# Two-block transformer kernel on one core: another order for the first transfers

## The chip, the cores and the metric

The kernel runs on one core of one Trainium2 chip. The metric is the device time of one execution in microseconds; three runs of the kernel before gave 947.91, 948.18 and 948.75 us, so the median is 948.18 us. A profile was taken of one further execution, which took 949.62 us; its recorded span is 947.6 us, and 2.0 us lie around the span.

## The reference

A sequence of 256 tokens with 1024 features goes through a first block and then through a second block of two layers, all in float32. Only the head of the first block matters for this change:

```
u = rms_norm(x, norm_g)                    # norm_g: the first of the "norm weights"
proj = u @ w_in                            # values v, queries q, keys k, convolution and gate columns
s = q k^T / 8 + alibi bias, softmax, times v   (16 heads)
y_conv = (silu(zc) * bg * conv3(cg * xc)) @ w_out_conv
gates  = sigmoid(g + b_merge)
h = x + (gate_c * y_conv + gate_a * y_attn) @ w_o ;  rms_norm(h, final_g)
```

The second block (memory attention, compressed, windowed and block attention with relative position bias, two convolutional feed-forward parts) follows, with further small tables: a one-hot of distances and the relative bias, the convolution taps of the feed-forward, the position embedding and the second matrix of the compression.

## The kernel before

Every weight comes as a block of 128 partitions by 1024 float32 (512 KB) out of one long tensor, `stream`. A block is loaded into a buffer `raw`, copied by ScalarE into a rounded upper part `wh` (`make_high`, L463), and VectorE writes the rest, `raw - wh`, into `wl` (`make_low`, L895). TensorE then makes three products for each pair: upper by upper, upper by lower, lower by upper. The activations are split in the same way into `xh` and `xl`. In this part of the kernel there are three `raw`, three `wh` and three `wl` buffers (RING = 3).

Nothing plans the order at run time: each engine has its own list of instructions, written out by hand, and semaphores tie them together. `split_l` counts the blocks that VectorE has split, `split_h` those that ScalarE has copied, `used` those that TensorE has finished. SyncE (SP) issues most transfers. It starts block b+3 when `split_l` says that block b has left its `raw` buffer. GpSimd (POOL) issues the bias of each head pair (`alibi`) and the norm's rows (`load_gb`).

The head of the program, in order:

- SP issues two halves of x (L311), the transposed norm weights `gbt` (L312), the first three weight blocks (L307), and seven small tables (L315 to L321): `convw` 16 KB, `bm` 8 KB, `onehot` 66 KB, `relb` 1.5 KB, `convf` 88 KB, `pe_kv` 16 KB, `w2` 128 KB. Each of the seven raises one semaphore, `consts_in`, by 16.
- TensorE warms up with products of zeros (L1720), transposes x (L1728), warms up again, and begins the stage "value rows": eight blocks, k = 0 to 7, each with four 512-column products of each kind (L1742, L1745, L1748).
- ScalarE squares x (L514), waits for `gbt`, and then rounds columns of the transposed x (`raw_high`, L523) between the copies of blocks 0, 1 and 2. Behind these stand L539 (a copy of a broadcast), the wait `consts_in >= 16 * 7` (L540), a small copy of the merge bias `bm` (L541), and only then the loop that copies block 3 and all later ones.
- VectorE scales the transposed x by `gbt` (`raw_fetch`, L1071), which is what `raw_high` reads.
- POOL makes the norm's reciprocal roots, issues the first bias (`alibi(0)`, L381) and the final norm's row (`load_gb(a["final_g"])`, L373), then waits for the finished values (L393).

TensorE also waits for all seven tables, but only behind the eight value blocks (L1760). The first bias is read by the first head pair's scores; the final row is read hundreds of microseconds later.

Of the kernel before, what the change touches and what calls it, by code (L numbers as in the profile page):

```python
# [47 lines left out]
RING = 3  # L48
# [47 lines left out]
def slot_of(b):  # L96
    if b in EXTRA:
        return EXTRA[b]
    return (b - sum(e < b for e in EXTRA)) % RING
# [14 lines left out]
B_DEEP = B_KM0  # L114


def home_of(b):

    if b < B_DEEP:
        return b % RING  # L120
    m = (b - B_DEEP) % DEEP
    return RING + m if m < RING else (B_DEEP + m) % RING
# [32 lines left out]
def build_program(nc, a):  # L155
    ctx = ExitStack()
    with ctx:
        def sb(name, shape, dt=F32):
            return ctx.enter_context(nc.sbuf_tensor("sb_" + name, shape, dt))

        def sem(name):
            return ctx.enter_context(nc.semaphore(name))
# [27 lines left out]
        gbt = sb("gbt", [P, 10, KT])  # L190
# [57 lines left out]
        split_h, split_l, used = sem("split_h"), sem("split_l"), sem("used")  # L248
        gains_in, kv_free = sem("gains_in"), sem("kv_free")
# [27 lines left out]
        def norm_wait(engine, nm, what, count):  # L277
            before = norms.index(nm) - first_norm.get(what, 0)
            engine.wait_ge(S[nm, what], before * per_norm[what] + count)
# [24 lines left out]
        @block.sync  # L304
        def _(sp):
            def load(b, home):
                sp.dma_start(raw[home][:, :, :], a["stream"][bass.ds(b, 1)].rearrange(  # L307
                    "a p (k c) -> p (a k) c", k=KT)).then_inc(landed[home], 16)

            for t in range(NT):  # L310
                sp.dma_start(x_tok[:, t, :], a["x"][0, t * P:(t + 1) * P, :]).then_inc(x_in[t], 16)  # L311
            sp.dma_start(gbt[:, :, :], a["gains_t"]).then_inc(gains_in, 16)  # L312
            for b in range(RING):
                load(b, slot_of(b))
            sp.dma_start(convw[:, :, :], a["conv_t"]).then_inc(consts_in, 16)  # L315
            sp.dma_start(bm[:, :, :], a["b_merge_t"]).then_inc(consts_in, 16)
            sp.dma_start(onehot[:, :], a["distance_hot"]).then_inc(consts_in, 16)
            sp.dma_start(relb[0:32, :], a["rel_bias_2"]).then_inc(consts_in, 16)
            sp.dma_start(convf[:, :, :, :], a["conv_f_t"]).then_inc(consts_in, 16)
            sp.dma_start(pe_kv[:, :, :], a["pe_t"]).then_inc(consts_in, 16)  # L320
            sp.dma_start(w2[:, :, :, :], a["w2_t"]).then_inc(consts_in, 16)  # L321

            with sp.Fori(1, B_DEEP // RING) as i:
                for n in range(RING):
                    sp.wait_ge(split_l, i * RING + (n - RING + 1))
                    load(i * RING + n, n)
            for b in range(B_DEEP // RING * RING, B_DEEP):
                sp.wait_ge(split_l, b - RING + 1)
                load(b, home_of(b))
            for b in range(B_DEEP, B_DEEP + DEEP):  # L330
                if b == B_DEEP:
                    sp.wait_ge(S["p2", "free_a"], KT // 2)
                if b == B_DEEP + 2:
                    sp.wait_ge(S["p2", "free_a"], KT)
                if b >= B_DEEP + RING:
                    sp.wait_ge(split_l, b - DEEP + 1)
                load(b, home_of(b))
            count = (N_BLOCKS - B_DEEP) // DEEP
            with sp.Fori(1, count) as i:
                for n in range(DEEP):  # L340
                    b = B_DEEP + n
                    sp.wait_ge(split_l, i * DEEP + (b - DEEP + 1))
                    load(i * DEEP + b, home_of(b))
            for b in range(B_DEEP + count * DEEP, N_BLOCKS):
                sp.wait_ge(split_l, b - DEEP + 1)
                load(b, home_of(b))
            for t in range(NT):
                norm_wait(sp, "n5", "z", 2 * t + 2)
                sp.dma_start(a["out"][0, t * P:(t + 1) * P, :], x_tok[:, t, :]).then_inc(out_done, 16)
            sp.wait_ge(out_done, 16 * NT)  # L350
# [3 lines left out]
        def _(pool):  # L354
# [9 lines left out]
            def rstd(nm, t, eps):  # L364

                norm_wait(pool, nm, "var", t + 1)
                chain.link(pool.tensor_scalar(st[:, 8 + t:9 + t], st[:, 6 + t:7 + t], 1.0 / D, eps,
                                              ALU.mult, ALU.add))
                pool.tensor_tensor(st[:, 10 + t:11 + t], st[:, 8 + t:9 + t], half[:, :],
                                   ALU.pow).then_inc(S[nm, "rstd"], 1)  # L370

            def load_gb(gain, shift):
                pool.dma_start(gb[:, 0, :], gain.partition_broadcast(P)).then_inc(gb_in, 16)  # L373
                if shift is not None:
                    pool.dma_start(gb[:, 1, :], shift.partition_broadcast(P)).then_inc(gb_in, 16)

            def alibi(i):

                if not isinstance(i, int) or i:
                    pool.wait_ge(S["p1", "max"], i * 4)  # L380
                pool.dma_start(bias[:, :, 0:T], a["alibi"][bass.ds(i, 1)].rearrange(  # L381
                    "a p (h c) -> p (a h) c", h=2)).then_inc(S["p1", "bias_in"], 16)

            for t in range(NT):
                rstd("n0", t, EPS_RMS)
            alibi(0)
            load_gb(a["final_g"], None)

            def pick_values(i):

                if not isinstance(i, int) or i:
                    pool.wait_ge(S["p1", "o"], i)
                pool.tensor_copy(v_s[:, :, :], v_all[:, :, bass.ds(i * P, P)]).then_inc(v_pair, 1)  # L393

            pool.wait_ge(v_up[0], 2)
            pick_values(0)

            pool.wait_ge(rel_sb, 1)
            pool.dma_start(rel_rows, relf[:, :]).then_inc(rel_out, 16)
# [57 lines left out]
        def _(act):  # L457
# [51 lines left out]
                                   accum_out=den[:, c:c + 1]).then_inc(S[ph, "exp"], 1)  # L509


            for t in range(NT):
                act.wait_ge(x_in[t], 16)
                act.activation(z[:, t, :], x_tok[:, t, :], ACT.Square,  # L514
                               accum_out=st[:, 6 + t:7 + t]).then_inc(S["n0", "var"], 1)
# [1048 lines left out]
        def _(pe):  # L1564
# [169 lines left out]
            def value_rows(k):  # L1734

                parts = [(xh[:, k, t * P:(t + 1) * P], xl[:, k, t * P:(t + 1) * P],
                          *(w[slot_of(k)][:, 4 * n:4 * n + 4, :].rearrange("p k c -> p (k c)") for w in (wh, wl)),
                          bank[4 + 2 * t + n]) for t in range(NT) for n in range(2)]
                pe.wait_ge(split_h, k + 1)
                norm_wait(pe, "n0", "xh", k + 1)  # L1740
                for th, _, hw, _, bk in parts:
                    pe.matmul(bk[:, :], th, hw, start=k == 0, stop=False)  # L1742
                norm_wait(pe, "n0", "xl", k + 1)
                for _, tl, hw, _, bk in parts:
                    pe.matmul(bk[:, :], tl, hw, start=False, stop=False)  # L1745
                ready(k + 1)
                for th, _, _, lw, bk in parts:
                    last = pe.matmul(bk[:, :], th, lw, start=False, stop=k == KT - 1)  # L1748
                last.then_inc(used, 1)
# [536 lines left out]
```

## Time and profile before

| | |
|---|---|
| median of 3 runs | 948.18 us (947.91 to 948.75) |
| profiled execution, its own time | 949.62 us |
| its span | 947.6 us |
| TensorE busy | 927.2 us, 98% |
| VectorE busy | 664.2 us, 70% |
| ScalarE busy | 529.2 us, 56% |
| GpSimd busy | 65.5 us, 7% |
| moved by DMA | 173.02 MB, mean 183 GB/s |

The busy shares are means over the whole span. The change touches only the first 36 us, so what counts is the order of events there: the chain of waits, the list of instructions by time, and the time from a transfer's issue to its landing.

### The profile page before, as it was taken

How to read it: one execution, taken by the hardware profiler on the slowest of the kernel's cores; microseconds unless marked ns; L12 is line 12 of the kernel's file. 1: busy time of each engine (PE TensorE's matmuls, PEld its weight loads, DVE VectorE, ACT ScalarE, POOL GpSimd, SP SyncE). 2: the span in 40 equal slices, each digit the busy share in tenths (PEclk: the TensorE clock that was granted, in tenths of full speed). 3: DMA queues.
4: the chain of work that ended last, by engine and by line, in shares of the span. 5: the costliest groups of instructions: out<-in, count | busy, mean ns of one | idle time of the engine just before them, and what ended most of it. 6: DMA issues, size and time to landing. Idle time of an engine off the chain costs nothing.

```text
span 947.6 us, 19722 instructions
## 1 busy us (share of the span) xinstructions
PE 927.2 (98%) x7025; PEld 845.9 (89%) x7030; DVE 664.2 (70%) x1286; ACT 529.2 (56%) x976; POOL 65.5 (7%) x116
## 2 busy tenths in 40 slices
PE   8999999999999999999999999999999999999995
PEld 6899999999999988667999999998988799999995
DVE  6666666566767877886786566677677886666666
ACT  6545555555544657764655455565665565555553
POOL 1000000000000002640000000001000100000001
PEclk9999999999999999999999999999999999999998
DMA  7655555557556565315366655555554546565641
GB/s 261 194 186 188 188 174 179 180 176 239 193 185 206 216 228 189 118 62 171 134 209 223 198 197 185 192 200 166 195 184 157 178 155 228 193 197 179 199 156 45
DMA packets 48235, 173.02 MB, mean 183 GB/s; under 512 B 6031, under 2 KB 6479, under 8 KB 48060
## 3 DMA queue, kind: packets, MB, share of 16 engines
q1 hardware_dynamic: 44732, 159.78, 50.4%
q0 software_dynamic: 3456, 12.61, 4.4%
q8 instruction: 30, 0.49, 0.2%
q14 instruction: 17, 0.14, 0.0%
HBM read 171.29 MB, written 1.07 MB: 182 GB/s over the span
## 4 chain that ended last, share of the span: by engine, by line
PE 89%; DVE 5%; ACT 3%; issue 1%; DMA 1%; POOL 0%; POOLq 0%; SPq 0%; DVEq 0%; ACTq 0%
PE bank L1575 18%; PE bank L1576 18%; PE bank L1574 18%; PE ysum L1645 6%; PE ysum L1647 6%; PE ysum L1646 6%; PE bank L1696 2%; DVE sb_wl L895 2%; PE ysum L1703 1%; PE ysum L1710 1%; ACT sb_wh L463 1%; PE ysum L1742 1%; PE ysum L1748 1%; PE ysum L1745 1%; PE ysum L1574 1%
## 5 line engine op out<-in xcount | busy, mean ns | idle before, releaser
L1575 PE MATMUL bank<-sb_xl,sb_wh 128*128 128x256 f32 x1360 | 378.1, 278 | 0.0
L1576 PE MATMUL bank<-sb_xh,sb_wl 128*128 128x256 f32 x1360 | 376.0, 276 | 0.0
L1574 PE MATMUL bank<-sb_xh,sb_wh 128*128 128x256 f32 x1332 | 370.7, 278 | 0.0
L895 DVE TENSOR_TENSOR sb_wl<-sb_raw,sb_wh 128x1024 fp32r<-128x1024 f32 x196 | 239.2, 1223 | 109.0 <-ACT sb_wh L463 107.6
L1576 PEld LDWEIGHTS bank<-sb_xh,sb_wl 128*128 128x128 f32 x1360 | 255.5, 188 | 0.0
L1575 PEld LDWEIGHTS bank<-sb_xl,sb_wh 128*128 128x128 f32 x1360 | 255.5, 188 | 0.0
L1574 PEld LDWEIGHTS bank<-sb_xh,sb_wh 128*128 128x128 f32 x1332 | 250.3, 188 | 5.0 <-issue 2.7
L463 ACT ACTIVATE sb_wh<-sb_raw 128x1024 fp32r<-128x1024 f32 x196 | 205.8, 1055 | 87.2 <-PE bank L1576 39.2
L895 DVE TENSOR_TENSOR sb_wl<-sb_gates,sb_wh 128x1024 fp32r<-128x1024 f32 x63 | 76.9, 1220 | 9.7 <-ACT sb_wh L463 9.7
L1645 PE MATMUL ysum<-sb_wh,sb_mh 128*128 128x512 f32 x208 | 81.3, 391 | 0.1
L1646 PE MATMUL ysum<-sb_wl,sb_mh 128*128 128x512 f32 x208 | 81.1, 390 | 0.0
L1647 PE MATMUL ysum<-sb_wh,sb_ml 128*128 128x512 f32 x208 | 81.0, 390 | 0.0
L463 ACT ACTIVATE sb_wh<-sb_gates 128x1024 fp32r<-128x1024 f32 x63 | 66.3, 1052 | 4.4 <-PE ysum L1626 2.3
L789 ACT ACTIVATE sb_t_a<-bank,sb_convf 128x256 f32<-128x256 f32 x44 | 24.9, 565 | 74.1 <-PE bank L1576 69.8
L1469 DVE SCALAR_TENSOR_TENSOR sb_t_a<-bank,sb_convf,sb_t_a 128x255 f32<-128x255 f32 x44 | 21.2, 482 | 43.1 <-ACT sb_t_a L789 43.1
L508 ACT ACTIVATE sb_pr<-sb_sc,sb_mx 128x128 f32<-128x128 f32 x80 | 35.4, 445 | 25.0 <-DVE sb_mx L1046 25.0
L895 DVE TENSOR_TENSOR sb_wl<-sb_t_dg,sb_wh 128x1024 fp32r<-128x1024 f32 x32 | 39.1, 1223 | 10.9 <-ACT sb_wh L463 10.9
L1647 PEld LDWEIGHTS ysum<-sb_wh,sb_ml 128*128 128x128 f32 x208 | 39.1, 188 | 8.3
L1645 PEld LDWEIGHTS ysum<-sb_wh,sb_mh 128*128 128x128 f32 x208 | 39.0, 188 | 8.2 <-issue 1.0
L1646 PEld LDWEIGHTS ysum<-sb_wl,sb_mh 128*128 128x128 f32 x208 | 39.0, 188 | 7.1
L463 ACT ACTIVATE sb_wh<-sb_t_dg 128x1024 fp32r<-128x1024 f32 x32 | 33.9, 1060 | 11.8 <-PE bank L1576 5.7
L1575 PE MATMUL bank<-sb_mixl,sb_wh 128*128 128x256 f32 x128 | 35.6, 278 | 0.0
(308 smaller groups left out, 1497.3 us busy)
## 6 DMA issues: line engine op xcount, KB each, us to landing
sb_raw<-in_stream SPq DMA_DIRECT2D x201, 512.0 KB, 3.4
sb_gates<-in_stream SPq DMA_DIRECT2D x66, 512.0 KB, 3.3
sb_t_dg<-in_stream SPq DMA_DIRECT2D x33, 512.0 KB, 4.2
sb_bias<-rel_rows POOLq DMA_DIRECT2D x12, 384.0 KB, 3.9
sb_bias<-in_alibi POOLq DMA_DIRECT2D x8, 256.0 KB, 3.1
sb_gb<-in_ln_g POOLq DMA_DIRECT2D x4, 512.0 KB, 4.9
sb_gb<-in_ln_b POOLq DMA_DIRECT2D x4, 512.0 KB, 7.2
sb_x_tok<-in_x SPq DMA_DIRECT2D x2, 512.0 KB, 3.7
```

Of the source, the lines that this page charges most:

```text
L463: act.activation(wh[slot_of(b) if slot is None else slot][:, :, :], raw[home_of(b)][:, :, :], ACT.Copy).then_inc(split_h, 1)
L508: act.activation(to[:, branch, h, cols], src, ACT.Exp, bias=mx[:, c:c + 1], scale=-1.0, accum_out=den[:, c:c + 1]).then_inc(S[ph, "exp"], 1)
L789: act.activation(t_a[:, :], bank[2 * c][:, 0:T], ACT.Identity, bias=convf[:, layer, bass.ds(i, 1), 3], scale=convf[:, layer, bass.ds(i, 1), 2]
L895: dve.tensor_tensor(wl[slot][:, :, :], raw[home_of(b)][:, :, :], wh[slot][:, :, :].bitcast(F32), ALU.subtract).then_inc(split_l, 1)
L1469: cf.link(dve.scalar_tensor_tensor(out=t_a[:, 1:T], in0=bank[2 * c][:, 0:T - 1], scalar=convf[:, layer, bass.ds(i, 1), 1], in1=t_a[:, 1:T] ...
L1574: pe.matmul(out, wh[slot][:, k, :], mov_h(k), start=k == 0, stop=False)
L1575: pe.matmul(out, wh[slot][:, k, :], mov_l(k), start=False, stop=False)
L1576: last = pe.matmul(out, wl[slot][:, k, :], mov_h(k), start=False, stop=k == KT - 1)
L1645: pe.matmul(out, th[:, t * P:(t + 1) * P], hw, start=start, stop=False)
L1646: pe.matmul(out, th[:, t * P:(t + 1) * P], lw, start=False, stop=False)
L1647: last = pe.matmul(out, tl[:, t * P:(t + 1) * P], hw, start=False, stop=stop)
L1696: last = pe.matmul(outs[h][:, cols], q[r, t * P:(t + 1) * P], k[r, 0:lead + (t + 1) * P], start=True, stop=True)
```

## The change

- The transfer of `gbt` leaves SP's list and becomes ScalarE's first instruction.
- SP's fourth, fifth and sixth weight loads are written out ahead of the loop (which now begins at 2 in place of 1), each with the same wait as before. The seven tables now stand between and behind them: `convw` and `bm` behind the fourth load, `onehot` and `relb` behind the fifth, `convf`, `pe_kv` and `w2` behind the sixth.
- POOL waits for `used >= 2` before it issues the first bias.
- POOL issues the final norm's row behind its first copy of values (L393) in place of before it.

The waits for `consts_in` (L540 and L1760) are as they were.

```
-            sp.dma_start(gbt[:, :, :], a["gains_t"]).then_inc(gains_in, 16)
             for b in range(RING):
                 load(b, slot_of(b))
+
+            sp.wait_ge(split_l, 1)
+            load(RING, 0)
             sp.dma_start(convw[:, :, :], a["conv_t"]).then_inc(consts_in, 16)
             sp.dma_start(bm[:, :, :], a["b_merge_t"]).then_inc(consts_in, 16)
+            sp.wait_ge(split_l, 2)
+            load(RING + 1, 1)
             sp.dma_start(onehot[:, :], a["distance_hot"]).then_inc(consts_in, 16)
             sp.dma_start(relb[0:32, :], a["rel_bias_2"]).then_inc(consts_in, 16)
+            sp.wait_ge(split_l, 3)
+            load(RING + 2, 2)
             sp.dma_start(convf[:, :, :, :], a["conv_f_t"]).then_inc(consts_in, 16)
             sp.dma_start(pe_kv[:, :, :], a["pe_t"]).then_inc(consts_in, 16)
             sp.dma_start(w2[:, :, :, :], a["w2_t"]).then_inc(consts_in, 16)
 
-            with sp.Fori(1, B_DEEP // RING) as i:
+            with sp.Fori(2, B_DEEP // RING) as i:
...
             for t in range(NT):
                 rstd("n0", t, EPS_RMS)
+            pool.wait_ge(used, 2)
             alibi(0)
-            load_gb(a["final_g"], None)
...
             pool.wait_ge(v_up[0], 2)
             pick_values(0)
+            load_gb(a["final_g"], None)
...
+            act.dma_start(gbt[:, :, :], a["gains_t"]).then_inc(gains_in, 16)
             for t in range(NT):
                 act.wait_ge(x_in[t], 16)
```

## Rows read from the trace of the kernel before

**Rows 1.** Page, part 1: busy us (share of the span) xinstructions, by engine.
```profile
PE 927.2 (98%) x7025; PEld 845.9 (89%) x7030; DVE 664.2 (70%) x1286; ACT 529.2 (56%) x976; POOL 65.5 (7%) x116
```

**Rows 2.** Waits of TensorE, whole span: us in total, times, longest.
```profile
PE ysum L1742 <- ACT sb_wh L463: 1.5, 1, 1.5
```

**Rows 3.** Chain that ended last, in order of time: start us, us, what.
```profile
2.26 6.75 DMA sb_raw<-in_stream
9.03 1.07 ACT sb_wh L463
10.14 1.21 PE ysum L1742 x4
...
18.21 0.92 PE ysum L1748 x4
19.13 0.91 PE ysum L1742 x4
20.05 0.92 PE ysum L1745 x4
```

**Rows 4.** Instructions in order of time, SP: start us, us, engine line op.
```profile
1.79 0.42 SPq L312 DMA_DIRECT2D sb_gbt<-in_gains_t  x1
...
6.15 0.49 SPq L319 DMA_DIRECT2D sb_convf<-in_conv_f_t  x1
...
7.22 0.45 SPq L321 DMA_DIRECT2D sb_w<-in_w_t  x1
11.52 47.08 SPq L307 DMA_DIRECT2D sb_raw<-in_stream  x18
```

**Rows 5.** Instructions in order of time, ScalarE and VectorE (brackets: idle before, releaser).
```profile
7.70 0.88 DVE L1071 TENSOR_SCALAR sb_pt<-bank,sb_gbt 128x256 f32<-128x256 f32 x2 [5.63 <-DMA sb_gbt<-in_gains_t]
...
14.97 1.22 DVE L895 TENSOR_TENSOR sb_wl<-sb_raw,sb_wh 128x1024 fp32r<-128x1024 f32 x1
...
15.95 0.20 ACT L541 ACTIVATE sb_bmh<-sb_bm 128x16 f32<-128x16 f32 x1
...
16.19 1.06 ACT L463 ACTIVATE sb_wh<-sb_raw 128x1024 fp32r<-128x1024 f32 x1
```

**Rows 6.** Instructions in order of time, TensorE's two warm-ups.
```profile
2.31 2.31 PE L1720 MATMUL bank<-sb_zeros 128*128 128x512 bf16 x5 [2.31 <-POOL sb_t_b L361]
...
7.36 1.24 PE L1720 MATMUL ysum<-sb_zeros 128*128 128x512 bf16 x5
```

**Rows 7.** DMA issues, 0 to 40 us: xcount, KB each, median us from issue to landing.
```profile
sb_raw<-in_stream SPq DMA_DIRECT2D x15, 512.0 KB, 4.3
...
sb_gb<-in_final_g POOLq DMA_DIRECT2D x1, 512.0 KB, 6.0
sb_bias<-in_alibi POOLq DMA_DIRECT2D x1, 256.0 KB, 5.8
...
sb_gbt<-in_gains_t SPq DMA_DIRECT2D x1, 40.0 KB, 5.9
rel_rows<-sb_sc POOLq DMA_DIRECT2D x1, 24.0 KB, 1.8
```

**Rows 8.** Weight loads alone: first three (0 to 4 us), then the sixth (15 to 17).
```profile
DMA to landing us min/median/max: 6.7/7.5/8.6
...
DMA to landing us min/median/max: 4.3/4.3/4.3
```

**Rows 9.** Busy by stretch: PE, PEld, DVE, ACT, POOL, granted PE clock, DMA share, GB/s.
```profile
6.00:7.00 1.00, 1.00 (x7) 1.00 (x6) 0.00 (x0) 0.74 (x2) 0.46 (x2) 1.00 0.89 334
...
940.00:942.00 2.00, 0.00 (x0) 0.00 (x0) 2.00 (x3) 0.36 (x2) 1.47 (x2) 1.00 0.00 0
942.00:943.00 1.00, 0.00 (x0) 0.00 (x0) 0.67 (x1) 0.00 (x0) 1.00 (x1) 0.55 0.00 0
```

**Rows 10.** Instructions in order of time, POOL, 5 to 50 us.
```profile
35.92 0.54 POOL L399 DMA_DIRECT2D rel_rows<-sb_sc  x1 [0.42 <-DVE sb_sc L1121]
45.45 0.73 POOL L381 DMA_DIRECT2D sb_bias<-in_alibi  x1 [8.98 <-DVE sb_mx L1046]
```

More of the change, by code:

```diff
@@ L311, in _ @@
                 sp.dma_start(x_tok[:, t, :], a["x"][0, t * P:(t + 1) * P, :]).then_inc(x_in[t], 16)
-            sp.dma_start(gbt[:, :, :], a["gains_t"]).then_inc(gains_in, 16)
             for b in range(RING):
                 load(b, slot_of(b))
+            sp.wait_ge(split_l, 1)
+            load(RING, 0)
             sp.dma_start(convw[:, :, :], a["conv_t"]).then_inc(consts_in, 16)
             sp.dma_start(bm[:, :, :], a["b_merge_t"]).then_inc(consts_in, 16)
+            sp.wait_ge(split_l, 2)
+            load(RING + 1, 1)
             sp.dma_start(onehot[:, :], a["distance_hot"]).then_inc(consts_in, 16)
             sp.dma_start(relb[0:32, :], a["rel_bias_2"]).then_inc(consts_in, 16)
+            sp.wait_ge(split_l, 3)
+            load(RING + 2, 2)
             sp.dma_start(convf[:, :, :, :], a["conv_f_t"]).then_inc(consts_in, 16)
@@ L321, in _ @@
             sp.dma_start(w2[:, :, :, :], a["w2_t"]).then_inc(consts_in, 16)
-            with sp.Fori(1, B_DEEP // RING) as i:
+            with sp.Fori(2, B_DEEP // RING) as i:
                 for n in range(RING):
@@ L385, in _ @@
                 rstd("n0", t, EPS_RMS)
+            pool.wait_ge(used, 2)
             alibi(0)
-            load_gb(a["final_g"], None)
             def pick_values(i):
@@ L396, in _ @@
             pick_values(0)
+            load_gb(a["final_g"], None)
             pool.wait_ge(rel_sb, 1)
@@ L509, in exps @@
                                    accum_out=den[:, c:c + 1]).then_inc(S[ph, "exp"], 1)
+            act.dma_start(gbt[:, :, :], a["gains_t"]).then_inc(gains_in, 16)
             for t in range(NT):
```

## The prediction

> **What bounds the kernel now.** I read the page first. TensorE is busy for 98% of the span [rows 1], so nearly everything that delays it reaches the end, and little else does. The list of its waits then shows only one that this change could shorten: 1.5 us before the first value product, put down to ScalarE's copy of weight block 0 [rows 2]. The chain of waits tells what stands behind it. Block 0's load is issued at 2.26 us and takes 6.75 us, ScalarE copies it from 9.03, and TensorE starts at 10.14 [rows 3]. From there the pieces join without a gap: the products of k = 2 end at 19.13, those of k = 3 begin there, and the lower products L1745 of k = 3 follow at 20.05 [rows 3]. So two questions decide. How much earlier than 10.14 does the stage begin, and does any engine that feeds it come late before its eight blocks are done? Anything further on is paced by TensorE and moves with it.
>
> The instructions in order of time show the second question's weak place. ScalarE's small copy of the merge bias (L541) runs at 15.95, and the copy of block 3 starts at 16.19, 0.24 us later [rows 5]. Ahead of L541 stands the wait for all seven tables. SP had issued the last of them, `w2`, at 7.22 [rows 4], so they were there in time. TensorE needs block 3 at 19.13; the copy ends at 17.25, so 1.9 us of slack cover it.
>
> **The start: the norm weights leave SP's queue.** SP spends 0.42 us on the issue of `gbt`, and with the gap 0.47 us pass until the first weight load, 1.79 to 2.26 [rows 3, 4]. That much block 0's issue moves forward. VectorE's 5.6 us wait for `gbt` [rows 5] goes too, but it isn't what ends last: ScalarE waited for block 0 after its first `raw_high`. The tables, 324 KB by the tile shapes, were issued from 3.68 to 7.7 us and shared the engines with the first three loads. These took 6.7, 7.5 and 8.6 us to land against a median of 4.3 over the head [rows 7, 8]. I call the gain of TensorE's start g.
>
> - Lower bound: -0.2, if block 0's landing is set by the bytes ahead of it (x and `gbt` are still moved first) and `gbt`'s small pieces now slow x.
> - Upper bound: 1.5, since TensorE's second warm-up ends at 7.36 + 1.24 = 8.60 [rows 6] and nothing of the stage can begin earlier (10.14 - 8.60).
> - I take 0.7: 0.47 for the issue and 0.2 for the two thirds of the tables that were moved before 9.0 us, some 200 KB, of which perhaps a third delayed block 0 at 334 GB/s [rows 9].
>
> The issue on ScalarE costs about as much as on SP, 0.4 us, and lies in the time in which ScalarE waits for x anyway.
>
> **The tables: what is late next.** In the new order `convf`, `pe_kv` and `w2` are issued behind the sixth load, and that waits until VectorE has split block 2. The wait on ScalarE (L540) still asks for all seven. Step by step, with g = 0.7:
>
> 1. VectorE's split of block 2 ended at 14.97 + 1.22 = 16.19 [rows 5]; now 15.5.
> 2. SP issues a load 0.2 us behind the split that frees its buffer (the split of block 0 follows its copy, 10.10 [rows 3] + 1.22 = 11.3; the load started at 11.52 [rows 4]): 15.7.
> 3. The load takes 0.35 of SP and a gap of 0.05; from the start of `convf` to the start of `w2` it is 7.22 - 6.15 = 1.07 us [rows 4]. So `w2` is issued at 17.2.
> 4. `w2` lands L later. Nothing in the trace shows a transfer of 128 KB by itself. The nearest rows are a 24 KB transfer, 1.8 us, and weight loads of 512 KB at 4.3 us [rows 7, 8]; these are the two ends. With the sixth load and three tables (744 KB) and the delayed first bias (256 KB, issued at nearly the same moment) 1.0 MB go out between 15.7 and the landing. At 334 GB/s [rows 9] that is 3.0 us of moving, with about 1 us before the first byte and 0.5 behind the last: 20.2. So L = 3.0, midway between the ends.
> 5. ScalarE: the bias copy, and 0.24 later the copy of block 3, 20.44 to 21.50 [rows 5].
> 6. TensorE starts 0.05 behind such a copy and its first piece from a stand took 1.21 us in place of 0.91 [rows 3]: L1745 of k = 3 at 21.55 + 1.21 = 22.75, where it was at 20.05.
>
> The sum is +2.7 us. In general it is L + 0.4 - g: the slack of 1.9 us is used up whatever L is, as the tables are issued so late.
>
> The Trainium skill, "DMA: Bandwidth & Descriptors", section "Anatomy of one DMA — SWDGE (gpsimd) path", gives a transfer a fixed part of about 2.0 us and its bytes at 436 GB/s. That is measured on GpSimd's path; for the 744 KB from the issue of the sixth load it would be an estimate of 3.7 us, the tables in at 19.4, and a sum of +1.9. The 24 KB row at 1.8 us agrees with the fixed part; the 512 KB rows at 4.3 (where it gives 3.2) are above it, and I stay with the rows.
>
> **Behind the stall** the queue on ScalarE is: block 3, scaled column 0, block 4, scaled column 1, and so on. ScalarE needs about 1.06 + 0.4 us and gaps for each pair against TensorE's 2.75 per block, and blocks 4 and 5 have landed by then, so it has caught up within one block. VectorE's split of block 3 ends at 22.8; TensorE wants it 1.9 us after its restart, at 23.4. SP's seventh load waits for that split and goes at 22.9; with 4.3 us it is there at 27.2 and is wanted at 28.7. I count nothing more.
>
> **The first bias and the final row.** The wait `used >= 2` ends at about 15.7, and behind it on POOL stand only the copy of values, just ahead of 35.92 [rows 10], and what follows. The first bias took 5.8 us to land [rows 7]; the next bias is asked for at 45.45, right after the first one's last reader [rows 10], so it has over 20 us of cover. Without that cover it would cost up to 5.8. The final row (512 KB, 6.0 us [rows 7]) is now issued about 35.5, puts 0.6 us ahead of the `rel_rows` transfer at 35.92 [rows 10], which is read only in the second block, and shares the engines with a weight load that has some 6 us from issue to use. Nothing, or at worst 1 us. Taking both out of 7.6 to 14.5 us speeds the fourth load, which nobody waits for now.
>
> **The sum against the times.** The profiled execution took 949.62 us; with +2.7 it is 952.3. The median stands 1.44 below the profiled one, so I expect 950.9.
>
> **The rivals.**
>
> - *The tables are fast, the start is good* (not slower). Place: the landing of `w2`. With L = 1.8 as the 24 KB transfer and g = 1.5 the same steps give +0.7, 948.9 us. For it: the loads are queued and `w2` may be moved beside them; the first loads' 6.7 us shows how crowded the start is. Against it: 512 KB stand ahead in the same queue. It decides where L - g falls below 1.5, or 2.2 us for L at g = 0.7. Chance 0.15. To be faster than before, L would have to be under g - 0.4, which no transfer here shows: 0.03, about 946.
> - *TensorE's clock falls in the new gap.* TensorE would stand from 18.4 to 21.5, 3.1 us. After its last matmul at 938.0 the granted clock is still 1.00 up to 942 and 0.55 in the next us [rows 9], that is, it falls to 1.2 GHz of 2.4 after some 4 us; after the 1.5 us gap at the start the products ran at full rate. Price: the first warm-up of 512-column products took 2.31 us for five, the second 1.24 [rows 6], so the slow stretch lasted between 2.3 and 5.05 us (until 7.36), and half of it is lost: 1.2 to 2.5 more, 952.1 to 953.4 us. Chance 0.08; the gap is shorter than the one that was seen to lower the clock. The Trainium skill, "TensorE: Matmul & The Clock Gate", Part 1, says that the throttled state is the default and activity releases it, which is what the two warm-ups show.
> - *The final row collides at 36 us*, where one weight load comes late: +1, 951.9 with the rest. 0.02.
>
> **Numbers.** The forecast has 0.72, of which 0.06 ends within 0.2%. A change of 0.2%, 1.9 us, is about the least that can be told from none. Slower by more: 0.66 + 0.08 + 0.02 = 0.76; within: 0.06 + 0.15 = 0.21; faster: 0.03. The forecast's own range runs from L = 2.0 at g = 1.0 (+1.4) to L = 4.3 at g = 0.4 (+4.3), 949.6 to 952.5. Taking in part of the fast rival and of the clock's, I give 949.1 to 952.6.
>
> **What would show it.** Right: in the profile after, ScalarE's L541 stands at 19 to 21 us with a wait for a table's transfer of 3 us or more before it, TensorE has one gap of about 3 us before the L1742 of k = 3, and its first L1742 starts at 9 to 9.8. Step 1 is wrong if that start stays at 10.1. Step 4 is wrong if L541 runs before 17.5. The whole is wrong if TensorE shows no gap between k = 2 and k = 3, or if a second gap follows at k = 6 or at 36 to 45 us.

## The result and the profile after

Six runs of the changed kernel took 951.13, 951.61, 953.60, 953.86, 954.29 and 954.85 us, median 953.73; six of the kernel before have a median of 948.46. The ratio is 1.0048 with a 95% interval of 1.0035 to 1.0062: slower by 3.3 to 5.9 us. The forecast was 950.9 with a range of 949.1 to 952.6, so the direction was right and the time lies 1.1 us above the range. Three executions of the experiments below took several times as long as the others (two of the kernel before, one of e10) and are left out of every range and ratio below and of e10's median.

The runs fall in two groups, and with them goes the mean granted clock of TensorE that each run lists: the share of full speed at which the engine was allowed to run, over the whole span. It is 0.997 in the two runs under 952 and 0.996 to 0.993 in the four above 953. The profiled execution is the fastest of the six (951.13 us, span 949.4), so by itself it shows only part of the loss. A second profile of the same kernel, taken in the experiments, was of the second group (954.58 us, span 952.8). Both are needed.

The page of the first, part 1 (busy us, share of the span, instructions); it answers to [rows 1]:

```profile
PE 927.1 (98%) x7030; PEld 844.7 (89%) x7030; DVE 664.3 (70%) x1286; ACT 529.0 (56%) x976; POOL 67.5 (7%) x116
```

The work of TensorE, VectorE and ScalarE is the same within 0.2 us; TensorE's weight loads show 1.2 us less and GpSimd 2.0 more. No engine on the chain does more work, so what was added is waiting. The waits of TensorE and of ScalarE from 12 to 24 us (us in total, times, longest):

```profile
PE ysum L1750 <- ACT sb_wh L470: 3.9, 2, 3.6
...
ACT sb_bmh L549 <- DMA sb_w<-in_w_t: 5.3, 1, 5.3
```

L1750, L1753 and L1756 are the three kinds of value products that were L1742, L1745 and L1748; L470 is the copy of a weight block, L549 the copy of the merge bias. The first line answers to [rows 2]: the 1.5 us wait has become 0.38 at the start and 3.56 ahead of k = 3. The second is new and names the cause, the landing of `w2`. The chain of waits of the same profile, in order of time, answers to [rows 3]:

```profile
1.33 4.54 DMA sb_x_tok<-in_x
...
13.44 1.15 DVE sb_wl L903
14.60 0.35 SPq L307
14.99 0.43 SPq L325
15.47 0.44 SPq L326
15.95 3.73 DMA sb_w<-in_w_t
19.71 0.23 ACT sb_bmh L549
19.96 1.06 ACT sb_wh L470
21.06 1.20 PE ysum L1750 x4
22.26 0.91 PE ysum L1753 x4
```

It reads as the forecast's steps 1 to 6, in their order. The split of block 2 ends at 14.59, the sixth load goes out at 14.60, the tables behind it, `w2` at 15.95; 3.73 us later ScalarE may copy the bias, then block 3, and TensorE goes on at 21.06. The lower products of k = 3 begin at 22.26, where they began at 20.05 [rows 3]: +2.2 us, of which the span keeps 1.8 (949.4 against 947.6).

At the front, the instructions in order of time show the first products starting 1.6 us before those of [rows 3], and the same block of k = 3 behind its gap (brackets: idle before, releaser):

```profile
8.52 1.20 PE L1750 MATMUL ysum<-sb_wh,sb_xh 128*128 128x512 f32 x4 [0.38 <-ACT sb_wh L470]
...
21.06 1.20 PE L1750 MATMUL ysum<-sb_wh,sb_xh 128*128 128x512 f32 x4 [3.56 <-ACT sb_wh L470]
```

### The profile page after: what moved, and what is told of

Its sections match the earlier page's. It is cut to its first block, busy times and chain, and to the rows that moved or that the text cites. A ratio compares the mean times of both kernels' runs of the same rounds, so it can differ in the third digit from the quotient of the medians.

```text
span 949.4 us, 19717 instructions
## 1 busy us (share of the span) xinstructions
PE 927.1 (98%) x7030; PEld 844.7 (89%) x7030; DVE 664.3 (70%) x1286; ACT 529.0 (56%) x976; POOL 67.5 (7%) x116
## 4 chain that ended last, share of the span: by engine, by line
PE 88%; DVE 6%; ACT 3%; issue 1%; DMA 1%; POOL 0%; SPq 0%; POOLq 0%; DVEq 0%; ACTq 0%
PE bank L1583 18%; PE bank L1584 18%; PE bank L1582 18%; PE ysum L1653 6%; PE ysum L1655 6%; PE ysum L1654 6%; DVE sb_wl L903 2%; PE bank L1704 2%; PE ysum L1711 1%; PE ysum L1718 1%; ACT sb_wh L470 1%; PE ysum L1582 1%; PE ysum L1583 1%; PE ysum L1584 1%; ACT sb_xh L503 1%
## 5 line engine op out<-in xcount | busy, mean ns | idle before, releaser
L470 ACT ACTIVATE sb_wh<-sb_raw 128x1024 fp32r<-128x1024 f32 x196 | 205.7, 1055 | 87.1 <-PE bank L1584 39.2
L470 ACT ACTIVATE sb_wh<-sb_gates 128x1024 fp32r<-128x1024 f32 x63 | 66.3, 1053 | 4.4 <-PE ysum L1634 2.3
L1477 DVE SCALAR_TENSOR_TENSOR sb_t_a<-bank,sb_convf,sb_t_a 128x255 f32<-128x255 f32 x44 | 21.2, 482 | 43.1 <-ACT sb_t_a L797 43.1
L470 ACT ACTIVATE sb_wh<-sb_t_dg 128x1024 fp32r<-128x1024 f32 x32 | 33.9, 1060 | 11.8 <-PE bank L1584 5.7
```

The costliest lines, as they stand in the source:

```text
L470: act.activation(wh[slot_of(b) if slot is None else slot][:, :, :], raw[home_of(b)][:, :, :], ACT.Copy).then_inc(split_h, 1)
L1477: cf.link(dve.scalar_tensor_tensor(out=t_a[:, 1:T], in0=bank[2 * c][:, 0:T - 1], scalar=convf[:, layer, bass.ds(i, 1), 1], in1=t_a[:, 1:T] ...
```

## The experiments

Theory C: the stall costs its length in every run, and in most runs the granted clock also falls in it. Rival T: the transfer of `w2` lands later in most runs than in the profiled one. All kernels below were timed beside the kernel before; its medians were 948.69 us (beside a0, e1, e2, e3), 948.63 (b0, e4, e5, e6) and 948.48 (e7 to e10). The last four were timed on another chip than the first eight, so a comparison across the two goes by the ratio to the kernel before as well as by the time.

### The changed kernel again (a0_again), no edit

> The changed kernel once more, unedited. Its six runs so far are 951.1, 951.6, 953.6, 953.9, 954.3 and 954.9 us with a mean granted clock of 0.997 in the first two and 0.993 to 0.996 in the others; its profile (951.13) has the gap of 3.6 us ahead of the k = 3 products and no lower clock in it. Theory C (clock): the gap costs 2.2 us net in every run, and in most runs the granted clock falls in the gap as well, which costs 2 to 3.5 us more. Then the runs fall in two groups, near 951 with clock 0.997 and near 954 with less, and a profile of the second kind shows slow products behind the gap. Theory T (transfer): w2 lands 2 to 3.5 us later in most runs than in the profiled one, and the clock has little to do with it. Then a profile near 954 shows a gap of 6 us or more.

Measured: median 954.70 us (953.92 to 955.09), ratio 1.0063 (1.0051 to 1.0075), clock 0.993 or 0.994 in all six. Theory C expected two groups again, near 951 and near 954; only the second was seen. The chain of its profile:

```profile
16.58 3.94 DMA sb_w<-in_w_t
20.78 1.06 ACT sb_wh L470
21.89 2.08 PE ysum L1750 x4
23.97 1.71 PE ysum L1753 x4
25.68 1.71 PE ysum L1756 x4
27.38 1.26 PE ysum L1750 x4
28.64 0.93 PE ysum L1753 x4
```

And busy times by stretch (PE, PEld, DVE, ACT, POOL, granted clock, DMA share, GB/s):

```profile
20.00:21.00 1.00, 0.00 (x0) 0.00 (x0) 0.00 (x0) 0.43 (x2) 0.00 (x0) 1.00 0.00 1
21.00:22.00 1.00, 0.11 (x1) 0.11 (x1) 0.13 (x1) 1.00 (x2) 0.00 (x0) 0.59 0.00 0
22.00:28.00 6.00, 6.00 (x14) 4.68 (x15) 5.38 (x9) 3.23 (x6) 0.00 (x0) 0.50 0.53 171
28.00:29.00 1.00, 1.00 (x6) 0.80 (x5) 0.49 (x1) 0.78 (x2) 0.00 (x0) 1.00 0.81 205
```

T falls: `w2` takes 3.94 us to land, as good as the 3.73 of the fast profile, and the gap is 3.75 us against 3.56. What differs is the clock, 0.50 (1.2 of 2.4 GHz) from 22 to 28 us. The piece of four products takes 1.71 us where it took 0.91. TensorE calls itself 100% busy in that stretch, with 14 products in 6 us; the stretch from 28 has 6 in one. Someone who reads busy shares alone sees no loss here.

### The wait behind the loop (e1_wait_behind)

```
-            act.wait_ge(consts_in, 16 * 7)
-            act.activation(bmh[:, :, :], bm[:, :, :], ACT.Copy, scale=0.5).then_inc(ach, 1)
...
             refill(0, KT - 1)
+            act.wait_ge(consts_in, 16 * 7)
+            act.activation(bmh[:, :, :], bm[:, :, :], ACT.Copy, scale=0.5).then_inc(ach, 1)
```

> The wait for the seven tables and the merge bias copy move behind the loop of blocks 3 to 10 on ScalarE. Both theories: no gap ahead of k = 3, and the earlier start of 1.6 us is all that is left. Block 3 and the later loads are there in time. 948.3 - 1.6 = 946.7 us, spread under 1 us, clock 0.997. If instead something else in the new order were late (the sixth load, the first bias, the final row), it would stay at 948 or above.

Measured: 947.93 us (947.22 to 948.45), ratio 0.9992 (0.9983 to 1.0001). One wait moved takes 6.8 us off the 954.70 of its neighbour. Its chain runs without a gap from 8.80 us on, and k = 3 begins at 17.79:

```profile
8.80 1.21 PE ysum L1750 x4
...
16.87 0.92 PE ysum L1756 x4
17.79 0.91 PE ysum L1750 x4
```

So the whole loss hangs on that wait. But the gain left is 0.8 us in the medians, with an interval that just holds none, and not the 1.6 that I expected from the two profiles; b0 below bears on why.

### Warm-ups in the gap (e2_filler)

```
                 value_rows(k)
+                if k == 2:
+                    norm_wait(pe, "n0", "xf_act", 2)
+                    warm_up(10)
```

> The changed kernel, with ten more warm-up products of zeros on TensorE between k = 2 and k = 3 (about 2.2 us at full rate, inside the gap of 3.6 us). Theory C: the clock stays up in every run, so all are near 951.0, none above 952, clock 0.997. Theory T: nothing is gained, runs from 951 to 955, median near 953.7.

Measured: 952.54 us (951.52 to 953.08), ratio 1.0038 (1.0024 to 1.0051), clock 0.997 or 0.998 in all. The transfer is no faster (3.92 us in its chain), the first products start at 9.11 like those of the neighbour (9.15), and still it is 2.2 us faster. The expected level, 951.0, was 1.5 too low, and one run lies above the 952 that was to be the limit: the level came from a profile with an early start (8.52). The same view as above:

```profile
18.00:21.00 3.00, 2.26 (x11) 0.82 (x10) 0.00 (x0) 0.49 (x2) 0.00 (x0) 1.00 0.55 179
21.00:22.00 1.00, 0.17 (x1) 0.17 (x2) 0.18 (x1) 1.00 (x3) 0.00 (x0) 1.00 0.00 0
22.00:28.00 6.00, 6.00 (x27) 4.91 (x28) 5.64 (x10) 3.96 (x7) 0.00 (x0) 1.00 0.51 171
```

27 products between 22 and 28 us against 14. No run of e2 is as slow as the fastest of a0. Products that compute nothing made the kernel faster than its neighbour.

### A longer gap (e3_longer_gap)

Two more squares on ScalarE ahead of the copy of block 3:

```
+            norm_wait(act, "n0", "var", 2)
+            for _ in range(2):
+                chain.link(act.activation(z[:, 1, :], x_tok[:, 1, :], ACT.Square))
```

> The changed kernel, with two more squares of x on ScalarE ahead of the copy of block 3, 2.5 us in all, so the gap is about 6.1 us. The output of these squares is overwritten later. Theory C: the clock falls in every run: 951.1 + 2.5 = 953.6, and 2 to 3.5 us for the slow stretch, 955.6 to 957.1 with a spread under 1 us, and the profile shows products of 0.43 us behind the gap. Theory T: the spread stays as wide as before, 953.6 to 957.4.

Measured: 956.00 us (955.02 to 957.26), ratio 1.0074 (1.0062 to 1.0087), clock 0.993 to 0.995 in all. The gap is 5.84 us:

```profile
22.00:23.00 1.00, 0.00 (x0) 0.00 (x0) 0.00 (x0) 0.99 (x1) 0.00 (x0) 0.60 0.00 0
23.00:29.00 6.00, 4.88 (x12) 3.81 (x13) 4.89 (x8) 3.87 (x6) 0.00 (x0) 0.50 0.34 107
29.00:30.00 1.00, 1.00 (x6) 0.83 (x5) 0.61 (x2) 0.56 (x1) 0.00 (x0) 0.99 0.93 344
```

The level fits C, but the spread of 2.2 us is wider than the 1 us I gave. 2.1 us more of gap cost 1.3 us more: the slow clock set in within the gap and covered 4.9 us of work here against 6.1 in a0, half of which difference is 0.6 us.

### The longer gap, filled (e10_long_filler)

The edits of e3 and e2 together, with `warm_up(20)`.

> The kernel with the longer gap (two more squares, 956.0), with 20 more warm-up products of zeros on TensorE in the gap (4.6 us). Theory C: the clock stays at 0.997 in all runs; what is left is the kernel with ten warm-ups in its gap (952.5) and the two squares (2.2): 954.7, none above 955.6, and no product behind the gap at half rate. Without an effect of the clock: 956.0.

Measured: 953.84 us (953.71 to 954.65) over five runs, ratio 1.0059 (1.0046 to 1.0073), against 956.00 and 1.0074 (1.0062 to 1.0087) unfilled. C's level was 954.7, so it is 0.9 lower still. It is the second pair of kernels that differ by nothing but idle or filled, but e3 was timed on the other chip, and the two intervals overlap; e2 against a0 is the pair that carries the argument. The clock is 0.996 or 0.997, and the profile shows no product at half rate:

```profile
18.00:24.00 6.00, 4.42 (x20) 1.85 (x20) 0.00 (x0) 3.38 (x5) 0.00 (x0) 1.00 0.28 82
24.00:30.00 6.00, 5.94 (x26) 4.91 (x27) 5.66 (x10) 4.08 (x8) 0.00 (x0) 1.00 0.51 158
```

### The last table apart (e6_w2_apart)

```
-            sp.dma_start(w2[:, :, :, :], a["w2_t"]).then_inc(consts_in, 16)
+            sp.dma_start(w2[:, :, :, :], a["w2_t"]).then_inc(w2_in, 16)
...
-            act.wait_ge(consts_in, 16 * 7)
+            act.wait_ge(consts_in, 16 * 6)
```

> The changed kernel, but w2 has a semaphore of its own, for which only TensorE waits, behind the value rows. ScalarE waits for the other six tables. The wait ends when pe_kv lands, issued 0.5 us before w2 and with 128 KB less: 0.5 to 1.2 us earlier. Theory C (clock falls only when the gap is long enough): a gap of about 2.6 to 3.1 us, the clock stays at 0.997 in most or all runs, 951.0 to 952.0, which is 3 us less than the changed kernel for 0.9 us of gap. Without such a step: 953.8.

Measured: 951.25 us (950.06 to 952.94), ratio 1.0031 (1.0019 to 1.0043). The wait ends at the landing of `pe_kv`, and the gap is 2.59 us (its timeline, brackets as before):

```profile
18.69 0.21 ACT L550 ACTIVATE sb_bmh<-sb_bm 128x16 f32<-128x16 f32 x1 [4.31 <-DMA sb_pe_kv<-in_pe_t]
...
20.05 1.19 PE L1751 MATMUL ysum<-sb_wh,sb_xh 128*128 128x512 f32 x4 [2.59 <-ACT sb_wh L471]
```

1.2 us less of gap went with 3.4 us against a0. Four runs lie between 950.06 and 951.25, three between 952.54 and 952.94. None has the 0.993 or 0.994 of a0; their clocks are 0.995 to 0.998, and 0.996 stands beside 950.27 as well as beside 952.94. By the mean clocks the full fall is gone, as expected, but the spread is not; what the three slower runs did stays open, as no profile caught one.

### The tables alone (e5_tables_only)

The kernel before, with the new order of SP's fourth to sixth load and of the tables, and nothing else of the change.

> The kernel before with one edit: the tables stand between and behind the fourth, fifth and sixth loads. The norm weights are on SP's queue, first bias and final row as before. If the tables are the whole cause of the slowdown: the wait ahead of the bias copy ends when w2 lands, the gap is 3.4 to 4.0 us, and the time is that of the changed kernel plus the lost start, 953.5 to 956.5, with the clock down to 0.993 or 0.994 in most runs. If the first bias beside w2 matters, the landing is under 3.5 us and the gap under 3.4, and the clock stays up in part of the runs: 951.5 to 953.

Measured: 953.62 us (952.52 to 955.22), ratio 1.0054 (1.0042 to 1.0066). The order of the tables makes a slowdown of 5.0 us by itself, against 5.3 and 6.0 with the whole change. Both columns of the expectation got something right: the time is the first's, the landing and the gap are the second's. The first bias, issued early here, is out of the way, and `w2` lands in 2.84 us:

```profile
18.01 2.84 DMA sb_w<-in_w_t
21.13 1.06 ACT sb_wh L470
```

The gap is 2.64 us. The clock is 0.997 in the fastest run (952.52) and 0.993 in the slowest (955.22), so at least one run of this kernel seems to have had the full fall; how long its own gap was isn't known, as the profile is of the fastest run. In the four between it is 0.996, which doesn't tell: kernels without a gap list 0.996 too (e9 with 948.1 us, for one).

### The norm weights alone, and back again (e4_gains_only, e7_gains_back)

e4 is the kernel before with `gbt` issued by ScalarE. e7 is e1 with `gbt` back on SP.

> The kernel before with one edit: the norm weights come from ScalarE's queue. The tables, first bias and final row stand as before. If the earlier start is due to this edit alone: 0.5 to 1.0 us faster, 947.7 to 948.2. If it needed the tables out of the way of the first loads: 948.5, no change; TensorE's start tells them apart (9.0 or below against 9.4).

> The changed kernel with the wait for the tables behind the loop of blocks 3 to 10 (as in the run that gave 947.9), and the norm weights back on SP's queue. If the start depends on which queue carries the norm weights: 0.5 us slower or more, 948.4 to 949.5, with TensorE's first value product at 9.3 or later. If the queue is worth nothing (the kernel before began at 8.64 in its second profile, with SP's queue): 947.9, within 0.3.

Measured: e4 948.31 us, ratio 0.9993 (0.9984 to 1.0002); e7 947.83 us, ratio 0.9996 (0.9987 to 1.0005). Neither can be told from the kernel before, nor e7 from e1. The edit reaches its transfer, though. In e4 `gbt` lands after 3.9 us, against 5.9 in [rows 7], but the two halves of x, which it now travels beside, land after a median of 4.1 us against 3.7 in the kernel before. (Over the profiles it is 4.1 in all eight with `gbt` on ScalarE's queue, and 3.6 to 4.1 in the six with it on SP's.)

```profile
sb_x_tok<-in_x SPq DMA_DIRECT2D x2, 512.0 KB, 4.1
...
sb_gbt<-in_gains_t ACTq DMA_DIRECT2D x1, 40.0 KB, 3.9
```

### GpSimd's edits alone, and the wait alone (e8_pool_only, e9_wait_only)

e8 is the kernel before with the later first bias and final row. e9 is the kernel before with only the wait and the bias copy moved as in e1.

> The kernel before with the two edits on GpSimd alone (first bias behind used >= 2, final row behind the first copy of values). In the second profile of the kernel before, the fourth weight load took 6.5 us beside these two transfers and TensorE stood 0.2 us ahead of k = 3. If that is usual, this gives 0.2 to 0.8 us: 947.9 to 948.4, and the fourth load lands in under 4 us. If not: 948.6.

> The kernel before with the wait for the tables and the bias copy moved behind the loop of blocks 3 to 10, nothing else. The tables are there in time before, so the wait costs nothing there: 948.6, within 0.3. If it were faster by 0.5 or more, the wait cost something before as well.

Measured: e8 948.33 us, ratio 0.9998 (0.9990 to 1.0007); e9 948.73 us, ratio 1.0000 (0.9991 to 1.0009). Both are worth nothing by time. In e8 the fourth load lands in 3.2 us; in e9, where the two transfers are early, in 5.6; with them early it is also 4.5 us in the first profile before, 4.7 in e4 and 6.5 in b0 below. In e8's profile the collision is gone, in a place where TensorE mostly didn't wait for it. e9 shows that the wait is free as long as the tables are issued ahead of it.

### The kernel before again (b0_before_again), no edit

> The kernel before once more, for a second profile. Its profiled execution of 949.62 us began the value rows at 10.14 us; the others took 948.18 to 948.8, about 1 us less. Theory S (start): in a usual execution block 0 lands earlier than in the profiled one, and TensorE begins at 9.1 to 9.5; then the change gives back only 0.3 to 0.9 us at the start and not 1.6, and the move of the wait alone (947.9) agrees with it. Rival: it begins at 10.1 here too, and the time between executions differs elsewhere.

One execution: 948.02 us, span 946.2. The first products start at 8.64, 1.5 us ahead of the first profile; then the fourth load takes 6.49 us and the block k = 3 begins at 17.73 (chain of waits):

```profile
7.62 0.98 ACT sb_wh L463
...
10.03 6.49 DMA sb_raw<-in_stream
16.62 1.07 ACT sb_wh L463
17.73 1.19 PE ysum L1742 x4
```

The rival falls, and theory S holds in the main, though this start lies before its 9.1 to 9.5. Nothing differs in the kernel, but the first three loads landed in 5.3, 6.1 and 7.2 us, where [rows 8] has 6.7, 7.5 and 8.6. Over the profiles with `gbt` on SP the first products start at 8.64, 8.89, 9.47, 9.66, 10.14 and 10.60 us, mean 9.57. With `gbt` on ScalarE's queue they start between 8.46 and 9.25 in eight profiles, mean 8.96. So the start is earlier by 0.6 us on average, about what I had taken for g, and the profile that I argued from had a late one. With a spread of 2 us within the first group the 0.6 is uncertain.

## Why the prediction failed where it did

- *What bounds the kernel, and the cause of the slowdown*: right. The chain after shows steps 1 to 6 in their order; e1 takes all of it away by moving the wait, e5 makes it by the order of the tables.
- *The start, g = 0.7*: 0.6 on average, within the spread of the starts, and 1.6 in the profiled pair, whose 8.52 lies ahead of the 9 to 9.8 that I named as the sign; a0's 9.15 lies in it. As a gain it is small in the times: 0.3 us in e4, whose interval holds zero. By my reason, SP's issue slot and the tables' bytes, it should have been seen in e4 and e7, and e7 shows nothing of the first.
- *Step 4, the landing of `w2`, L = 3.0*: too short. It is 3.73, 3.94, 3.92, 4.00 and 3.92 us in the five profiles with the full change, and 2.84 without the first bias beside it. The bytes were wrong, not the rate: from the issue of the sixth load to the landing of `w2` the engines moved 1.24 MB in 5.1 us, a mean of 243 GB/s, where step 4 has 1.0 MB in 4.5 us with its 1.5 us at the two ends, a mean of some 230. (Those two ends stand in no row of before. In the first profile after, 0.9 us pass from the issue of x at 0.88 to the first bytes, and 0.4 us from the last bytes, at 19.3, to the landing of `w2`.) The surplus was issued earlier and still on its way: the rest of the fifth load, issued at 12.34, and of the tables behind it:

```profile
14.60:19.70 5.10, 2.91 (x13) 2.06 (x11) 1.98 (x6) 0.00 (x0) 0.93 (x1) 1.00 0.70 243
```

  The term was under-sized by 0.7 to 1.0 us. In the first profile the early start hid it: the sum there came to +2.2, and the profiled time, 951.13 us, is in the range by that luck. With L = 3.9 and g = 0.6 the forecast's formula, L + 0.4 - g, gives +3.7; e2, where the clock stays up, measured 952.54 - 948.69 = +3.85. On the 948.46 of the kernel before, +3.7 is 952.2, still inside the range; what took the median out of it is the next term.
- *The rival "TensorE's clock falls in the new gap"*: here the prediction failed, as its sum has this term at nothing. I gave it 0.08 with the words "the gap is shorter than the one that was seen to lower the clock". With the gap at 3.1 us by my steps and 3.6 to 3.8 by the traces, the mean clock shows the fall (0.993 or 0.994) in eight of the twelve runs of this kernel; two more at 0.996 took 953.60 and 953.86 us and may have had a shorter one. Its price was worth 2.2 us in the medians (954.70 against 952.54) and 2.8 at the place (6.75 us for the four pieces from 21.89 in a0, 3.95 for the same four in e2); I had written 1.2 to 2.5, from the slow stretch at the start, at most 5.05 us. The one in a0 lasted 6.8 us, from the 0.59 of the stretch 21 to 22 us, that is about 21.2, to 28.0.
- *The error in reading* was to take one row, the tail of the kernel, where the engine was done at 938.0 and the clock was 1.00 up to 942, for a threshold. In a0 TensorE ended its products of k = 2 at 18.14, so the clock fell after 3.0 us of idle. In e3 that was some 3.9 us, and some 4.1 at the tail that I read. In the first profile of the changed kernel it had not fallen after 3.56:

```profile
21.00:22.00 1.00, 0.94 (x4) 0.80 (x5) 0.95 (x1) 1.00 (x3) 0.00 (x0) 1.00 0.00 0
```

  So the length of the gap alone doesn't decide: the clock stayed up through more idle in one execution than was enough in another of the same kernel. One fall seen is no measure of the shortest gap that can have one.
- *First bias and final row*: the cover held, TensorE has no wait from 28 to 60 us in the first profile; the final row was issued at 39.8 us, later than my 35.5, and cost nothing seen. The bias's bytes were in the forecast and its price is about those bytes: in e5, without it beside `w2`, the engines moved 1.03 MB in 4.25 us, also at 242 GB/s, and L is 2.84. The 0.21 MB that are missing make 0.9 us at that rate. This is one profile of a kernel that also starts later, so it fits the cause without proving it.
- *Budget of the +6.0 us of a0*: stall 3.85, clock 2.16. This takes e2 for a0 without the fall. In the first six runs, with two of them free of it, the median moved 5.3. The clock's 2.8 at the place and 2.2 in the medians differ by 0.6; e2's chain loses about 0.4 us between 219 and 247 us that a0's doesn't. What makes that isn't settled.

The best versions seen (e1, 947.93, and e7, 947.83) undo the slowdown by moving one wait, and can't be told from the kernel before.

## What to carry to other kernels

- When transfers are put later, look for each wait on their shared semaphore, and above all for waits that count all of a group when the next instruction needs one: here 16 * 7 for a copy that reads 8 KB. Move the wait with the transfer.
- A gap on TensorE of some 3 us has two prices, its length and, in some executions, a slow stretch behind it (in a0 it set in after 3.0 us of idle). Give the second its own likelihood, and ask the mean clock of each run for it, not one profile.
- One profile of a start that is bound by transfers may be 1 us off the usual one. Where the forecast is 1 or 2 us, hold the profiled execution's own time against the median first; here it was 1.44 above, and b0, with its start 1.5 us earlier, took 1.6 us less.

## What was not expected of the hardware

- The clock fell in a gap of 3.75 us, 3.0 us after the last product, and then stayed at 0.50 under uninterrupted products from 22 to 28 us, 14 of them. In another execution it stayed at 1.00 through a gap of 3.56 us. With ten products of zeros in the gap it stayed at 1.00, and no run's mean clock was under 0.997.
- A 128 KB transfer issued 1.35 us behind a 512 KB load took 3.7 to 4.0 us to land with a 256 KB transfer of GpSimd beside it, and 2.8 in the one profile without.
- The 40 KB of norm weights landed in 3.9 us whenever they came from ScalarE's queue beside x. From SP's queue behind x it was 3.8, 4.3, 4.5, 4.7, 5.9 and 6.4 us, with the same instructions ahead of its issue.
